# One hybrid encoder layer on one Trainium2 core: orders in the VectorE and ScalarE queues of the gated-attention stage and of the merge

## The chip, the cores and the metric

One core of a Trainium2 chip. The metric is the device time of one execution in microseconds (us), lower is better. TensorE is called PE in the profile, its weight loads PEld; VectorE is DVE, ScalarE is ACT, GpSimd is POOL; SyncE (SP) issues most of the transfers.

## The reference

One layer over 1088 tokens (1024 of a prompt, 64 of a running stream) of width 1024. The three branches share one projection of the normalised input; only branches B and C and the merge are touched here.

```python
u = rmsnorm(x, g) @ w_in            # q, k, v, low-rank gate, output gate r, memory q, merge gates
# B: gated linear attention, 4 heads, dk=64, dv=128, blocks of 64 tokens
b = cumsum(log_a); q_d = q*exp(b); k_d = k*exp(-b); k_e = k*exp(b_last - b)
o = tril(q_d @ k_d.T) @ v + q_d @ S
S = exp(b_last) * S + k_e.T @ v     # from block to block
o_gla = rmsnorm_per_head(o) * g * silu(r)
# C: softmax attention of 4 heads x 128 into 256 memory tokens; K, V = rmsnorm(mem) @ w
h = x + w_out( sum over 3 branches of sigmoid(gate_n) * (o_n @ w_branch[n]) )
# then a router, two experts of 32 for each token (top 2 of 8 in the best of 4 groups), final rmsnorm
```

All products run in fp32 accuracy. A large product takes three passes: each operand is split into a high part (a copy on ACT, `w_high`, `x_high`) and a low part (a subtraction on DVE, `w_low`), and PE adds low x high, high x low and high x high (`three_pass`, L68).

## The kernel before

The kernel is a chain of stages, each with five instruction queues written out by hand and tied by counting semaphores (`wait_ge`, `then_inc`); a queue runs strictly in the order in which it is written. This case touches the joint stage of branches B and C (from 358 to 733 us of the profiled execution) and the start of the merge stage (from 733 us).

**Joint stage.** The four heads of branch B are done as two pairs p = 0 and 1. Columns of the projection come in blocks of 128 (`BLOCKS`: q, k, v, v for each pair, then r0 to r3, then mq, mk, mv for each memory head), and each block b is split into units of 384, 384 and 320 tokens (`units`, 0 to 40 and more). A unit is 24 matmuls of PE into one half of `gproj`; it waits until DVE has the low half of its weights (`g_low`, by `w_low(b)`) and until ACT has emptied the unit two before it (`drained`). ACT's `take` drains units, and after the last unit of block b it splits the high half of block b + 2 (`w_high`, L1140); after the last unit of an r block it also runs `sigmoid`, three activations over 1088 columns (L1218 to L1222). DVE's `w_low` is L1314.

For each pair ACT's `grow(p)` (L1187 to L1193) turns the scanned log-decay into three tiles `tt`, `la`, `bs` and the block factors `dec`; DVE's `gate_q` (L1338) and `gate_k` (L1344, L1346) multiply them into q and k, giving `qd`, `kd` and `ke`. PE transposes `ke` and v (`turn`, L949), DVE copies the results out (L1356). Then `stream(p)` runs t = 0 to 8 over tiles of 128 tokens: `pair` (L962) and `update` (L973) on PE for t + 1, DVE's `mask` (L1367) and `advance` (L1380), and `attend` (L987, L993). Units of later blocks are threaded between them by `PRE`, `MID` and `POST`; for pair 1: unit 30, the column sums `squares` (L1001) and unit 31 at t = 4, unit 32 after it; unit 33 at t = 6; unit 34, squares, unit 35 at t = 8. Before each `squares` ACT must `evacuate` the outputs (L1199) and square them (L1205); after it `root` (L1210, L1213) and DVE's `norm` (L1388) finish the head norm. `silu(h)` on DVE (L1394, L1397) uses the sigmoid of r; drains of r2 and r3 wait for the `silu` of r0 and r1, whose tiles they overwrite. The memory rows are normalised by `memory_norm` on ACT and DVE (L1431), transposed on PE by `memory_rows` (L1027) behind stream(1), split by `memory_high` (L1247) and `memory_low` (L1437); behind `memory_rows` PE goes on with unit 36 (block 12, the first memory query).

Queue order before, as far as it is touched:

- ACT: stream(0), grow(1), unit 18's drain, ...; in stream(1) each sigmoid directly after the last drain of its r block, so sigmoid(0) at t = 1, sigmoid(1) at t = 3, sigmoid(2) at t = 4, sigmoid(3) at t = 8 in front of `w_high(13)`; memory_norm at t = 2 and 3; then evacuate(1, 2) and memory_high.
- DVE: stream(0) ending in norm(0, 1), then w_low(7), gate_q(1), gate_k(1); in stream(1) silu(0), silu(1), silu(2) at t = 3, 4, 6, memory_norm at t = 6, 7, norm(1, 1) at its end; then memory_low, w_low(12), w_low(13).
- grow(1) also waits until all state updates of pair 0 are done, since both pairs use one tile `dec`.

**Merge stage.** Step i = 0 to 23 covers branch n = i // 8 and 128 output columns: PE's `gate(i)` (three groups of 24 matmuls, `bank<-xhi,...`) and `part(i)` (three groups of 12), DVE's `weigh(i, g)` (L2230), ACT's `sigmoid(i)` (L2045, one activation for each group). The gate of step 0 was computed in the joint stage. PE runs gate(1), part(0), part(1), gate(2), part(2), ...; gate(2) waits for DVE's w_low(2) and for sigmoid(1), which empties its banks. In ACT's queue sigmoid(1) stands behind `w_high(2)` (L2025) and `wb_high(2)` (L2030), and wb_high(2) waits for a transfer that SP issues only when part(0) is done (L1722). At the same time POOL writes 8 MB of zeros to `expert_rows` (16 transfers of 512 KB, L1767).

Of the kernel before, what the change touches and what calls it, by code (L numbers as in the profile page):

```python
# [13 lines left out]
F32 = mybir.dt.float32  # L14
# [4 lines left out]
ACT = mybir.ActivationFunctionType  # L19
# [57 lines left out]
def build(nc, io, stop_after=99):  # L77
# [709 lines left out]
    G, E = [la, bs], [tt, qr]  # L787
    SM = CON + 2560
    NCH = T // CH
    dec = at("dec", [P, NCH], F32, SM)  # L790
    gnt = at("gnt", [P, 4], F32, SM + 96)
    bat = at("bat", [P, 2], F32, SM + 128)
    cmask = at("cmask", [P, P], I32, SM + 192)
    w2c = [at("w2c", [RANK, P], F32, off) for off in (SM + 704, CON + 512)]
    PRE = [{4: [14], 8: [16]}, {4: [30], 8: [34]}]
# [3 lines left out]
    with ExitStack() as own, Stage(nc) as ctx:  # L799
# [335 lines left out]
        def _(act):  # L1135
# [49 lines left out]
            def grow(p):  # L1185
                act.wait_ge(scanned, p + 1)
                nc.scalar.activation(tt[:, :], bs[:, :], ACT.Exp, scale=1.0 / TAU)  # L1187
                if p:
                    act.wait_ge(advanced, NCH)
                nc.scalar.activation(dec[:, :], blk(bs[:, :])[:, :, CH - 1], ACT.Exp, scale=1.0 / TAU)  # L1190
                nc.scalar.activation(la[:, :], la[:, :], ACT.Exp, scale=1.0 / TAU)
                act.drain()
                nc.scalar.activation(bs[:, :], bs[:, :], ACT.Exp, scale=-1.0 / TAU).then_inc(grown, 1)  # L1193
# [30 lines left out]
            def take(js):  # L1224
                for j in js:
                    drain(j)
                    b = units[j][0]
                    if j + 1 == done[b]:
                        if BLOCKS[b][0] == "r":
                            sigmoid(BLOCKS[b][1])  # L1230
                        if b + 2 < len(BLOCKS):
                            w_high(b + 2)

            def memory_norm(t):
                act.wait_ge([row0, row1][t], 16)
# [33 lines left out]
            def stream(p):  # L1269
                for t in range(NT):  # L1270
                    if t in (4, 8):
                        evacuate(p, t // 4 - 1)
                    take(PRE[p].get(t, []))
                    if t in (4, 8):
                        root(p, t // 4 - 1)
                    take(MID[p].get(t, []))
                    take(POST[p].get(t, []))
                    if p and t in (2, 3):
                        memory_norm(t - 2)
                if p == 0:  # L1280
                    evacuate(p, 2)

            w_high(0)
            w_high(1)
# [5 lines left out]
            softplus(1)  # L1290
            take(range(9, 13))
            stream(0)
            grow(1)
            take([18])
            root(0, 2)
            take(range(19, 24))
            stream(1)
            evacuate(1, 2)
            for t in range(2):
                memory_high(t)  # L1300
            take([36])
            root(1, 2)
            take(range(37, 41))
# [4 lines left out]
        def _(ve):  # L1308
# [29 lines left out]
                nc.vector.tensor_tensor(qd[:, :], qr[:, :], tt[:, :], ALU.mult).then_inc(qd_ready, 1)  # L1338

            def gate_k(p):  # L1340
                ve.wait_ge(drained, first["k", p] + 3)
                if p:
                    ve.wait_ge(paired, NT)
                nc.vector.tensor_tensor(kd[:, :], ke[:, :], bs[:, :], ALU.mult).then_inc(kd_ready, 1)  # L1344
                ve.drain()
                nc.vector.tensor_tensor(ke[:, :], ke[:, :], la[:, :], ALU.mult).then_inc(ke_ready, 1)  # L1346
# [23 lines left out]
            def advance(p, t):  # L1370
                ve.wait_ge(updated, 9 * p + t + 1)
                if t == FULL:
                    ve.wait_ge(st_in, 16 * p + 16)
                if p and t == 0:
                    ve.wait_ge(stored, 32)
                for u in range(rows_of(t) // CH):
                    c = 2 * t + u
                    src, dst = (c, c + 1) if c < 16 else (17, 18)
                    ve.drain()
                    nc.vector.scalar_tensor_tensor(out=S[:, dst, :], in0=S[:, src, :], scalar=dec[:, c:c + 1],  # L1380
                                                   in1=half(ub, u)[:, 0:P], op0=ALU.mult, op1=ALU.add).then_inc(advanced, 1)

            def norm(p, g):
# [23 lines left out]
            def stream(p):  # L1407
                mask(p, 0)
                advance(p, 0)
                for t in range(NT):  # L1410
                    if t + 1 < NT:
                        mask(p, t + 1)
                        advance(p, t + 1)
                    if t == 4 and p == 0:
                        w_low(6)
                    if p:
                        if t in (2, 4):
                            w_low(9 + t // 2)
                        if t in (3, 4, 6):
                            silu({3: 0, 4: 1, 6: 2}[t])  # L1420
                    if t == 5:
                        norm(p, 0)
                    if p and t in (6, 7):
                        memory_norm(t - 6)
                norm(p, 1)

            def memory_norm(t):
                ve.wait_ge(mrooted, t + 1)
# [74 lines left out]
                copy(0, kind, g)  # L1503
            w_low(5)
            stream(0)
            w_low(7)
            gate_q(1)
            gate_k(1)
            for kind, g in (("k", 0), ("k", 1), ("k", 2)):
                copy(1, kind, g)  # L1510
            w_low(8)
# [4 lines left out]
            stream(1)  # L1516
            for t in range(2):
                memory_low(t)
            w_low(12)
            w_low(13)  # L1520
            silu(3)
            norm(1, 2)
            w_low(14)
# [138 lines left out]
    with Stage(nc) as ctx:  # L1662
# [358 lines left out]
        def _(act):  # L2021
# [74 lines left out]
            for i in range(LEAD):  # L2096
                if i % KC == 0:
                    o_split(i // KC)
                if i:
                    w_high(i + 1)  # L2100
                wb_high(i + 1)
                if LEAD - 2 <= i:
                    wo_split(2 * (i - LEAD + 2))
                    wo_split(2 * (i - LEAD + 2) + 1)
                if i:
                    sigmoid(i)
            w_high(LEAD + 1)
            wb_high(LEAD + 1)
# [477 lines left out]
```

## Time and profile before

| | |
|---|---|
| median of 3 runs | 1951.29 us (1948.56 to 1953.52) |
| the profiled execution | 1949.11 us, its span 1947.5 us |
| PE busy | 1784.2 us (92% of the span), 10344 matmuls |
| DVE, ACT, POOL busy | 1105.5 us (57%), 874.9 us (45%), 193.4 us (10%) |
| mean granted PE clock | 0.961 of full speed |
| transfers | 326.57 MB, mean 168 GB/s |

The span in 40 slices of 48.7 us, busy share in tenths; the joint stage lies in slices 8 to 15, the merge begins at slice 16:

```profile
PE   7998898899998998999999999969999999999960
...
DVE  4328777443234542223233335557888988898857
ACT  4215545323243432112121223236887788778832
...
PEclk9999999899999998999999999979999999999985
```

Timeline rows read: start in us, duration (of a merged run of xN instructions, first start to last end), engine, line, operation, output <- inputs, shapes; in brackets the idle time in front of it and what ended it.

### The profile page before, as it was taken

What the parts mean: (1) busy time and instruction counts of PE and PEld (TensorE: products, weight loads), DVE (VectorE), ACT (ScalarE), POOL (GpSimd) and SP (SyncE); (2) the same over time, 40 slices, a digit from 0 to 9 for tenths busy, and PEclk for the clock granted to TensorE, in tenths of its full rate; (3) what the DMA queues carried; (4) which work ended last, traced back from release to release, by engine and by line L of the source; (5) the groups of instructions that cost most, each with busy time, mean ns of one, the idle gap of its engine ahead of it and who ended that gap; (6) DMA issues with size and microseconds to landing.
All of it is one profiled execution on the core that took longest, in us unless ns stands there. A gap on an engine that the chain in (4) does not pass through costs nothing. (4 is left out here: it accounts for less than half of the span.)

```text
span 1947.5 us, 25714 instructions
## 1 busy us (share of the span) xinstructions
PE 1784.2 (92%) x10344; PEld 1570.7 (81%) x10344; DVE 1105.5 (57%) x1343; ACT 874.9 (45%) x1128; POOL 193.4 (10%) x189
## 2 busy tenths in 40 slices
PE   7998898899998998999999999969999999999960
PEld 5877777687977877999999998857888888888850
DVE  4328777443234542223233335557888988898857
ACT  4215545323243432112121223236887788778832
POOL 0004445100000003000000000000000000000003
PEclk9999999899999998999999999979999999999985
DMA  4210000111101217111112142149999999999947
GB/s 173 81 58 24 23 23 1 46 33 48 44 25 55 82 39 220 49 49 44 39 49 88 47 148 76 71 160 349 417 410 415 415 417 408 417 415 411 403 159 273
DMA packets 131719, 326.57 MB, mean 168 GB/s; under 512 B 8576, under 2 KB 84176, under 8 KB 107024
## 3 DMA queue, kind: packets, MB, share of 16 engines
q1 hardware_dynamic: 116096, 269.40, 37.0%
q0 software_dynamic: 10896, 38.74, 5.5%
q10 hardware_dynamic: 4608, 16.78, 2.1%
q8 instruction: 84, 1.38, 0.3%
q14 instruction: 35, 0.29, 0.0%
HBM read 285.01 MB, written 39.87 MB: 167 GB/s over the span
## 5 line engine op out<-in xcount | busy, mean ns | idle before, releaser
L2320 DVE TENSOR_TENSOR low<-raw,hig 128x2048 fp32r<-128x2048 f32 x192 | 431.5, 2286 | 68.1 <-ACT hig L2092 67.7
L2092 ACT ACTIVATE hig<-raw 128x2048 fp32r<-128x2048 f32 x192 | 359.5, 1915 | 21.9 <-ACT ye L2160 14.2
L1945 PE MATMUL bank<-hig,xel 128*128 128x512 f32 x512 | 204.4, 399 | 3.9 <-DVE xel L2387 3.9
L1947 PE MATMUL bank<-hig,xeh 128*128 128x512 f32 x512 | 201.6, 394 | 0.0
L1946 PE MATMUL bank<-low,xeh 128*128 128x512 f32 x512 | 200.9, 392 | 0.0
L71 PE MATMUL bank<-xhi,glo 128*128 128x384 f32 (+1 forms) x552 | 181.3, 329 | 9.5 <-ACT sg L2045 7.8
L72 PE MATMUL bank<-xlo,ghi 128*128 128x384 f32 (+1 forms) x552 | 181.2, 328 | 0.0
L73 PE MATMUL bank<-xhi,ghi 128*128 128x384 f32 (+1 forms) x552 | 181.1, 328 | 0.0
L71 PE MATMUL gproj<-xhi,glo 128*128 128x384 f32 (+1 forms) x408 | 142.4, 349 | 10.1 <-DVE glo L1314 10.1
L73 PE MATMUL gproj<-xhi,ghi 128*128 128x384 f32 (+1 forms) x408 | 136.9, 335 | 0.0
L72 PE MATMUL gproj<-xlo,ghi 128*128 128x384 f32 (+1 forms) x408 | 136.8, 335 | 0.0
L672 DVE TENSOR_TENSOR_SCAN sfx<-sfx 128x1024 f32<-128x1024 f32 (+8 forms) x68 | 116.7, 1739 | 4.3 <-ACT sfx L547 4.1
L1945 PEld LDWEIGHTS bank<-hig,xel 128*128 128x128 f32 x512 | 97.6, 191 | 23.6 <-DVE xel L2387 4.5
L1947 PEld LDWEIGHTS bank<-hig,xeh 128*128 128x128 f32 x512 | 96.9, 189 | 20.7
L1946 PEld LDWEIGHTS bank<-low,xeh 128*128 128x128 f32 x512 | 97.3, 190 | 19.2
L71 PEld LDWEIGHTS bank<-xhi,glo 128*128 128x128 f32 x552 | 104.4, 189 | 9.9 <-issue 9.9
L284 POOL TENSOR_TENSOR att<-att,sfx 128x1023 f32<-128x1023 f32 (+8 forms) x68 | 98.6, 1461 | 117.3 <-DVE sfx L672 87.7
L2234 DVE TENSOR_TENSOR tm<-sg,bank 128x384 f32<-128x384 f32 (+1 forms) x42 | 22.3, 532 | 153.9 <-PE bank L73 153.9
L1971 PE MATMUL bank<-hig,htl 128*128 128x512 f32 x256 | 103.3, 403 | 1.4 <-DVE htl L2393 1.4
L73 PEld LDWEIGHTS bank<-xhi,ghi 128*128 128x128 f32 x552 | 104.5, 189 | 0.0
L72 PEld LDWEIGHTS bank<-xlo,ghi 128*128 128x128 f32 x552 | 104.4, 189 | 0.0
L1973 PE MATMUL bank<-hig,hth 128*128 128x512 f32 x256 | 100.6, 393 | 0.0
(403 smaller groups left out, 3630.5 us busy)
## 6 DMA issues: line engine op xcount, KB each, us to landing
raw<-in_w_e_gate_dram SPq DMA_DIRECT2D x64, 1024.0 KB, 8.0
raw<-in_w_e_up_dram SPq DMA_DIRECT2D x64, 1024.0 KB, 8.3
raw<-in_w_e_down_dram SPq DMA_DIRECT2D x64, 1024.0 KB, 7.5
graw<-in_w_in_dram SPq DMA_DIRECT2D x40, 512.0 KB, 3.6
expert_rows<-ye ACTq DMA_DIRECT2D x32, 512.0 KB, 8.2
xt<-in_x_prompt_dram SPq DMA_DIRECT2D x16, 512.0 KB, 3.6
expert_rows<-nil POOLq DMA_DIRECT2D x16, 512.0 KB, 10.3
braw<-in_w_branch_dram SPq DMA_DIRECT2D x24, 256.0 KB, 2.7
```

Source lines behind the costliest of these rows:

```text
L71: nc.tensor.matmul(out, wl, xh, start=(i == 0), stop=False)
L72: nc.tensor.matmul(out, wh, xl, start=False, stop=False)
L73: last = nc.tensor.matmul(out, wh, xh, start=False, stop=(i == len(parts) - 1))
L284: nc.gpsimd.tensor_tensor(att[n][:, 0:k - 1], att[n][:, 0:k - 1], sfx[n][:, 1:k], ALU.mult).then_inc(weighed, 1)
L672: nc.vector.tensor_tensor_scan(v, v, v, 1.0, ALU.mult, ALU.bypass).then_inc(scanned, 1)
L1945: nc.tensor.matmul(bank[:, :], xel[n % 2][:, kk, :], wh[:, k, :], start=(kk == 0), stop=False)
L1946: nc.tensor.matmul(bank[:, :], xeh[n % 2][:, kk, :], wl[:, k, :], start=False, stop=False)
L1947: last = nc.tensor.matmul(bank[:, :], xeh[n % 2][:, kk, :], wh[:, k, :], start=False, stop=(kk == KC - 1))
L1971: nc.tensor.matmul(bank[:, :], htl[n % 2][:, kk, :], wh[:, k, cols], start=(kk == 0), stop=False)
L1973: last = nc.tensor.matmul(bank[:, :], hth[n % 2][:, kk, :], wh[:, k, cols], start=False, stop=(kk == 3))
L2092: nc.scalar.activation(hig[q % HI][:, :], raw[q % RAW][:, :], ACT.Copy).then_inc(high, 1)
L2320: nc.vector.tensor_tensor(low[q % RAW][:, :], raw[q % RAW][:, :], hig[q % HI][:, :].bitcast(F32), ALU.subtract).then_inc(lowed, 1)
```

## The change

`dec` gets a slot for each pair and grow(1) loses its wait; grow(1) moves from behind stream(0) into it, at t = 4. On DVE gate_k(1) comes first behind stream(0), then norm(0, 1), gate_q(1), w_low(7). In stream(1) the sigmoids come at t = 1, 4 (between unit 31's and unit 32's drains) and 5, the fourth behind memory_high; ACT's memory_norm at t = 5 and 6; DVE's silu at t = 3, 6, 7, w_low(12) at t = 7, memory_norm at t = 7, 8, and norm(1, 1) behind w_low(13). In the merge w_high(2) and sigmoid(1) are issued in step 0, in front of wb_high(2).

```diff
-    dec = at("dec", [P, NCH], F32, SM)
-    gnt = at("gnt", [P, 4], F32, SM + 96)
-    bat = at("bat", [P, 2], F32, SM + 128)
+    dec = at("dec", [P, 2, NCH], F32, SM)
+    gnt = at("gnt", [P, 4], F32, SM + 160)
+    bat = at("bat", [P, 2], F32, SM + 1216)
...
-                if p:
-                    act.wait_ge(advanced, NCH)
-                nc.scalar.activation(dec[:, :], blk(bs[:, :])[:, :, CH - 1], ACT.Exp, scale=1.0 / TAU)
+                nc.scalar.activation(dec[:, p, :], blk(bs[:, :])[:, :, CH - 1], ACT.Exp, scale=1.0 / TAU)
...
-                    if j + 1 == done[b]:
-                        if BLOCKS[b][0] == "r":
-                            sigmoid(BLOCKS[b][1])
-                        if b + 2 < len(BLOCKS):
-                            w_high(b + 2)
+                    if j + 1 == done[b] and b + 2 < len(BLOCKS):
+                        w_high(b + 2)
...
+                    if p and t == 4:
+                        sigmoid(1)
                     take(POST[p].get(t, []))
-                    if p and t in (2, 3):
-                        memory_norm(t - 2)
-                if p == 0:
-                    evacuate(p, 2)
+                    if p == 0 and t == 4:
+                        grow(1)
+                    if p and t in (1, 5):
+                        sigmoid(t // 2)
+                    if p and t in (5, 6):
+                        memory_norm(t - 5)
+                evacuate(p, 2)
...
             stream(0)
-            grow(1)
...
             stream(1)
-            evacuate(1, 2)
             for t in range(2):
                 memory_high(t)
+            sigmoid(3)
             take([36])
...
             def gate_k(p):
+                ve.wait_ge(grown, p + 1)
...
+                        if t == 7:
+                            w_low(12)
-                        if t in (3, 4, 6):
-                            silu({3: 0, 4: 1, 6: 2}[t])
+                        if t in (3, 6, 7):
+                            silu({3: 0, 6: 1, 7: 2}[t])
                     if t == 5:
                         norm(p, 0)
-                    if p and t in (6, 7):
-                        memory_norm(t - 6)
-                norm(p, 1)
+                    if p and t in (7, 8):
+                        memory_norm(t - 7)
...
             stream(0)
+            gate_k(1)
+            norm(0, 1)
+            gate_q(1)
             w_low(7)
-            gate_q(1)
-            gate_k(1)
...
             for t in range(2):
                 memory_low(t)
-            w_low(12)
             w_low(13)
+            norm(1, 1)
             silu(3)
...
-                if i:
+                if i >= 2:
                     w_high(i + 1)
                 wb_high(i + 1)
...
-                if i:
+                if i == 0:
+                    w_high(2)
+                    sigmoid(1)
+                elif i >= 2:
                     sigmoid(i)
```

## Rows read from the trace of the kernel before

**Rows 1.** Waits of TensorE (PE), 355 to 860 us: reader <- writer: total, times, longest us.

```profile
PE gproj L71 <- DVE glo L1314: 12.0, 5, 7.2
PE bank L71 <- ACT sg L2045: 7.8, 1, 7.8
PE gupd L949 <- DVE ke L1346: 4.1, 1, 4.1
PE gout L1001 <- ACT osq L1205: 3.6, 1, 3.6
...
PE gout L1046 <- DVE pT L1462: 2.8, 2, 2.0
```

**Rows 2.** Windows, TensorE alone: us, busy (instructions), granted clock, DMA share, GB/s.

```profile
486.00:549.00 63.00, 60.59 (x426) 1.00 0.15 43
...
766.00:768.00 2.00, 2.00 (x8) 0.50 1.05 384
...
726.00:727.00 1.00, 0.68 (x5) 1.00 0.00 0
```

**Rows 3.** Timeline of ScalarE (ACT), 463 to 479 us: start, us, instruction [idle before <-releaser].

```profile
463.73 1.03 ACT L1199 ACTIVATE o_gla<-gout 128x1024 f32<-128x1024 f32 x1 [6.57 <-PE gout L993]
...
473.34 0.44 ACT L1175 ACTIVATE ke<-gproj 128x320 f32<-128x320 f32 x1 [1.27 <-PE gproj L73]
...
475.18 1.10 ACT L1187 ACTIVATE tt<-bs 128x1088 f32<-128x1088 f32 x1
...
477.47 1.11 ACT L1193 ACTIVATE bs<-bs 128x1088 f32<-128x1088 f32 x1
```

**Rows 4.** Timeline of VectorE (DVE), 472 to 485 us.

```profile
472.11 1.42 DVE L1388 SCALAR_TENSOR_TENSOR o_gla<-o_gla,gnt,osq 128x512 f32<-128x512 f32 x2 [9.21 <-ACT osq L1213]
...
481.21 1.29 DVE L1346 TENSOR_TENSOR ke<-ke,la 128x1088 f32<-128x1088 f32 x1
...
483.48 1.20 DVE L1356 COPY ken<-gupd 128x384 f32<-128x384 f32 x2 [0.98 <-PE gupd L949]
```

**Rows 5.** Timeline of PE, 485 us: column sums of pair 0, last group.

```profile
484.85 0.95 PE L1001 MATMUL gout<-osq,ones 128*128 128x64 f32 x4
```

**Rows 6.** Timeline of ACT, 543 to 553 us.

```profile
543.46 0.44 ACT L1175 ACTIVATE bs<-gproj 128x320 f32<-128x320 f32 x1 [3.59 <-PE gproj L73]
...
551.05 1.06 ACT L1205 ACTIVATE osq<-o_gla 128x1024 f32<-128x1024 f32 x1
```

**Rows 7.** Timeline of PE, 560 to 582 us.

```profile
560.83 0.61 PE L987 MATMUL gout<-atm,gvn 128*128 128x128 f32 x4
...
579.96 1.88 PE L1001 MATMUL gout<-osq,ones 128*128 128x512 f32 x4
```

**Rows 8.** Timeline of PE, 595 to 602 us.

```profile
595.17 0.69 PE L71 MATMUL gproj<-xhi,glo 128*128 128x384 f32 x1 [7.15 <-DVE glo L1314]
...
601.03 0.55 PE L1001 MATMUL gout<-osq,ones 128*128 128x64 f32 x4
```

**Rows 9.** Timeline of PE, 764 to 785 us, merge stage.

```profile
764.72 0.66 PE L71 MATMUL bank<-xhi,glo 128*128 128x384 f32 x1 [7.81 <-ACT sg L2045]
...
784.69 0.34 PE L71 MATMUL bank<-xhi,glo 128*128 128x384 f32 x1
```

**Rows 10.** Timeline of ACT, 763 to 777 us, merge stage.

```profile
763.57 0.63 ACT L2030 ACTIVATE bhi<-braw 128x512 fp32r<-128x512 f32 x1 [21.78 <-DMA braw<-in_w_branch_dram]
...
775.50 1.06 ACT L2025 ACTIVATE ghi<-graw 128x1024 fp32r<-128x1024 f32 x1 [10.22 <-DMA graw<-in_w_in_dram]
```

**Rows 11.** Timeline of DVE, 776 us, merge stage.

```profile
776.59 1.22 DVE L2208 TENSOR_TENSOR glo<-graw,ghi 128x1024 fp32r<-128x1024 f32 x1 [9.97 <-ACT ghi L2025]
```

**Rows 12.** Timeline of SyncE's DMA issues (SPq), 784 to 803 us, merge stage.

```profile
784.89 0.37 SPq L1722 DMA_DIRECT2D braw<-in_w_branch_dram  x1
...
796.75 0.37 SPq L1713 DMA_DIRECT2D graw<-in_w_in_dram  x1
...
802.69 0.37 SPq L1722 DMA_DIRECT2D braw<-in_w_branch_dram  x1
```

More of the change, by code:

```diff
@@ L1379, in advance @@
                     ve.drain()
-                    nc.vector.scalar_tensor_tensor(out=S[:, dst, :], in0=S[:, src, :], scalar=dec[:, c:c + 1],
+                    nc.vector.scalar_tensor_tensor(out=S[:, dst, :], in0=S[:, src, :], scalar=dec[:, p, c:c + 1],
                                                    in1=half(ub, u)[:, 0:P], op0=ALU.mult, op1=ALU.add).then_inc(advanced, 1)
```

## Prediction

> **What bounds the kernel now.** I read the page first: PE is busy 92% of the span, so time can be won only where PE stands still or runs at the lower clock. The waits of PE from the joint stage into the merge come next [rows 1]: four of them are single holes of 3.6 to 7.8 us, released by DVE's `ke`, ACT's `osq`, DVE's `glo` and ACT's `sg`; the other waits there are 2 us or less. The windows say what a hole costs beside itself [rows 2]: after the one of 7.8 us the granted clock is 0.50 (1.2 GHz), while behind an idle time of 2.0 us in the last memory head, and through 63 us with only small waits, it stayed at 1.00 (2.4 GHz). Last I read the timelines of ACT and DVE around each hole, to see what stood in the queue in front of the releasing instruction. In each sum, x is the moment that PE would reach with the change, on the clock of the old trace.
>
> The prices that recur: an activation over 1088 columns 1.1 us, so a sigmoid of three with its drains or `grow` some 3.4 us (475.18 to 478.58 [rows 3]); a DVE multiply over 1088 columns 1.29 us and two norms 1.42 us [rows 4]; `w_low` 1.22 us [rows 11]; `w_high` 1.06 us [rows 10]; a gate of 1088 columns 11.86 us and a part 5.94 us [rows 12], so a unit of 384 columns 11.86 x 384 / 1088 = 4.19 us.
>
> **Term a, the gates of pair 1.** PE has finished unit 18 at 478.4 (`ke` ready at 481.21 + 1.29 = 482.5, less the hole of 4.1 [rows 1, 4]). In front of `ke` stand grow(1) on ACT and norm, w_low(7), gate_q and kd on DVE. grow(1) moves into ACT's idle 6.57 us before evacuate(0, 1), which begins at 463.73 [rows 3]: it fits with 3.1 us to spare, and its scan lies in front of pair 0's whole stream in DVE's queue. Giving `dec` a second slot costs nothing; it only removes the wait. gate_k(1) then waits for the last k drain alone, 473.34 + 0.44 = 473.8 [rows 3], and `ke` is ready at 473.8 + 2 x 1.29 + 0.1 = 476.5, 1.9 us before PE wants it. What is late next: the third transpose group needs DVE's first copy, which now stands behind norm, gate_q and w_low(7), 1.42 + 1.29 + 1.22 less small overlaps: the copy starts at 480.3 where it started at 483.48 [rows 4]. That leaves a hole of some 1.5 us at 479.2, of the size that did not cost the clock. The gain is 3.2 us, plus 0.4 us for the column sums (0.95 us [rows 5] where the same form took 0.55 us [rows 8]), plus my estimate of 0.5 us for the transposes and first matmuls, which ran at the lower clock too. **4.1 us**; bounds 2.5 (the clock falls all the same) and 4.6.
>
> **Term b, the first column sums of pair 1.** PE went on at 551.05 + 1.06 = 552.1 after a hole of 3.6 us, so unit 30 ended at 548.5 [rows 1, 6]. In front of that square ACT had sigmoid(1), w_high(11), memory_norm(1) and the evacuation copy. With the sigmoid gone to after unit 31's drain, and the memory norm to t = 6, ACT drains unit 29 by 543.9 [rows 6], splits until 544.9, copies and squares until 547.1: 1.4 us before PE wants it. Then x = 548.5 + 1.88 (sums at full clock [rows 7]) + 4.19 (unit 31) = 554.6, where attend(4) began at 560.83 [rows 7]. **6.3 us**; bounds 0, if the 1.4 us are not there, and 6.5.
>
> What moves behind it must stay covered. By the same durations laid behind one another, sigmoid(0) ends near 532 and its silu near 542, before unit 30's drain needs it at 548.5. sigmoid(1) ends 3.4 us after unit 31's drain, near 558.5 on PE's new time; silu(1) stands behind mask(7) and advance(7), and ends near 566.4, while unit 33, whose drain needs it, ends near 567.3. sigmoid(2), memory_norm on both engines and w_low(12) follow in the holes; the mrow transposes are reached near 579.4 and their norms end near 573.6. No SP issue moves except by PE's own progress, and POOL's queue is untouched.
>
> **Term c, unit 36.** PE stopped at 595.17 - 7.15 = 588.0 and reached the next column sums at 601.03 [rows 8]; the unit alone takes 4.19 us, so 1.7 us of the 13.0 were the lower clock. The hole is a chain behind unit 35's drain: sigmoid(3) 3.4 us, w_high(13) 1.06, evacuation, four memory_high, four memory_low, w_low(12). w_low(12) now runs at t = 7 on DVE, more than 10 us before unit 36, and unit 36 needs nothing else of the chain. The three units of block 12 (11.9 us) then cover memory_high and memory_low (about 5 us), w_low(13) 1.2, norm(1, 1) 1.4 and silu(3). x = 588.0 + 4.2 = 592.2. **8.8 us**; bounds 5 and 9.
>
> **Term d, the merge.** PE stopped at 764.72 - 7.81 = 756.9 [rows 9]. sigmoid(1) stood behind wb_high(2), whose weights landed at 763.57 [rows 10]. Issued before it, sigmoid(1) waits only for weigh(0, g) and ends near 752; wb_high(2), now behind it, waits for the same transfer as before. gate(2) and part(2) then run from 756.9 to 756.9 + 11.86 + 5.94 = 774.7. What is late next is gate(3)'s weight block: landed at 775.50 [rows 10], low half ready at 776.59 + 1.22 = 777.8 [rows 11]. Its transfer is issued when part(0) is done, before anything changes, so it does not come earlier. gate(3) begins at 777.8 instead of 784.69 [rows 9]: 6.9 us. The new hole of 3.1 us lies between 2.0 (clock kept) and 3.6 us (sums of 3.78 us for 1.88, clock lost); nearest the latter, so I charge it what the old hole cost: 784.69 - 764.72 - 17.80 = 2.2 us. **4.7 us**; bounds 0 and 6.9.
>
> A rule of the Trainium skill would give another result here. The row shows that behind wb_high(2)'s block (763.57) the 512 KB of gate(3) took 12 us more, some 44 GB/s, while all queues together moved 384 [rows 2, 10]. DMA: Bandwidth & Descriptors, Queues, rings and completion order, says that each DMA engine takes the queue rows with work in turn, packet by packet. With an even share, 192 GB/s, the block would land 2.7 us after 763.57, gate(3) would not wait, and term d would be 7.8 + 2.2 = 10.0 us. The trace speaks against the even share, and I keep 4.7.
>
> **The sum.** 4.1 + 6.3 + 8.8 + 4.7 = 23.9 us. The profiled execution took 1949.11 us, so 1925.2; it lies 2.2 us under the median 1951.29, and against the median I get 1927.4 us. What follows (rest of the merge, router, experts) is released by PE's progress and moves forward whole; its first weights are ordered by PE's counts, not by a clock. A measurement of this kernel tells 0.3%, 5.9 us, from no change.
>
> **Rivals.**
> 1. One covered step is not covered. Term b has 1.4 us to spare, silu(1) has 0.9 us before unit 33's drain (and 1.5 us more before squares(1, 1) would feel it). If one fails by enough to take a hole of over 3 us, about 6 us are lost: 1933.5. For: the slacks are thin. Against: they are sums of steady durations. 0.15.
> 2. The merge gives nothing back: gate(3)'s transfer lands later, or the hole moves whole to gate(3): 1951.3 - 19.2 = 1932.1. 0.06.
> 3. The even share of the rule above: 1927.4 - 5.3 = 1922.1. For: only the rule. Against: rows 10. 0.04.
> 4. The saved time is not on the path: what bounds the later stages is their weight stream, and the stage's end only waits there. 1951. Against: those loads begin only when PE's projections of the merge are done. 0.05.
> 5. Slower: without its rests PE runs densely through the stage and is granted 1.2 GHz for longer. The first matmul of a gate took 0.66 us at 0.50 and 0.34 us at 1.00 [rows 2, 9]; at half the clock a stretch of dense work takes up to twice its time. It decides from some 30 us of work at that level, which cost the 24 gained and the 5.9 that a measurement tells; over the 55 us of PE work between the holes of terms b and c and the first memory head it would be 55 us: 1982. Against: the 63 us before the hole of term b ran at 1.00 with PE busy for 60.6 of them [rows 2]. 0.03.
>
> The forecast itself has 0.67. The range 1921 to 1935 takes in rivals 1 to 3 and the bounds of terms a and d; it leaves out 4, 5 and a failure of two terms. Faster by over 0.3%: 0.92; within: 0.05; slower: 0.03.
>
> **What would show it.** In the changed kernel's waits of PE: `ke` gone or under 0.5 us, `ken` at about 1.5 us, `osq` gone, the 7.15 us of `glo` gone, `sg` gone, and a new `glo` L2208 hole of about 3 us at gate(3) with the clock at 0.50 behind it. The joint stage should be 19 us shorter (358 to 733 before), gate(4) should begin 4.7 us earlier in the merge, and everything after should keep its length. Wrong if an `osq` or `bs` drain wait of over 3 us appears near 545 to 575, or if gate(3)'s wait is near 8 us or missing.

## The result and the profile after

The changed kernel takes 1925.3 us (median of 4 runs, 1921.16 to 1928.22) against 1951.2 us: ratio 0.9864, interval 0.9846 to 0.9883, so 26.5 us faster (22.8 to 30.0). The profiled execution took 1926.25 us, its span 1924.8 us, the mean granted clock is 0.967 (0.961 before).

The waits of PE from 355 to 860 us, to be read against [rows 1] (reader <- writer: total, times, longest in us):

```profile
PE gproj L71 <- DVE glo L1313: 4.9, 4, 2.9
...
PE bank L71 <- ACT sg L2047: 3.4, 1, 3.4
PE gout L1046 <- DVE pT L1463: 2.9, 2, 2.0
...
PE gupd L949 <- DVE ken L1356: 2.1, 2, 1.7
```

`ke` and `osq` are gone. What is left of `glo` (L1313 is the old L1314) is 2.9 us at the stage's start, before anything that the change touches, and three small ones. New are 1.7 us at `ken`, inside the 2.1, and 3.4 us at `sg` where 7.8 stood. That label does not say that sigmoid(2) is the cause: it stands in ACT's queue behind the splits of gate(3)'s and part(3)'s weights, and the timelines below show that ACT itself had waited for a transfer.

Pair 1's gates on DVE, the queue of [rows 4] in its new order:

```profile
473.02 1.29 DVE L1344 TENSOR_TENSOR kd<-ke,bs 128x1088 f32<-128x1088 f32 x1 [10.94 <-ACT ke L1175]
...
478.14 1.22 DVE L1313 TENSOR_TENSOR glo<-graw,ghi 128x1024 fp32r<-128x1024 f32 x1
...
479.28 1.01 DVE L1356 COPY ken<-gupd 128x384 f32<-128x384 f32 x2
```

`kd` starts when k has been drained, and `ke` (behind it, at 474.41) is ready at 475.7, before PE goes over from unit 18 to the transposes at 477.45. The copies of the transposed `ke` begin at 479.28, behind w_low(7); that is the new hole. On PE (the rows of the third transpose group, the column sums of pair 0 and 1, attend(4), and the sums behind unit 36):

```profile
479.98 0.52 PE L949 MATMUL gupd<-ident,ke 128*128 128x128 f32 x3 [1.71 <-DVE ken L1356]
...
480.33 0.56 PE L1001 MATMUL gout<-osq,ones 128*128 128x64 f32 x4
...
546.41 1.88 PE L1001 MATMUL gout<-osq,ones 128*128 128x512 f32 x4
...
552.29 0.61 PE L987 MATMUL gout<-atm,gvn 128*128 128x128 f32 x4
...
583.51 0.55 PE L1001 MATMUL gout<-osq,ones 128*128 128x64 f32 x4
```

To be compared with [rows 5, 7, 8]: the sums at 480.33 take 0.56 us for 0.95; the sums of pair 1 run at 546.41 without a wait, in 1.88 us; from there to attend(4) it is 5.9 us, before it was 12.2 from the end of unit 30; and the sums behind unit 36 come 4.2 us after the last memory transposes, before 13.0.

The merge, against [rows 9 to 12], in four timelines: ACT's weight splits for part(2) and gate(3); DVE's low half for gate(3); PE's start of gate(3); and SP's issues when part(1), part(2) and gate(3) are done.

```profile
745.93 0.63 ACT L2032 ACTIVATE bhi<-braw 128x512 fp32r<-128x512 f32 x1 [11.48 <-DMA braw<-in_w_branch_dram]
...
758.07 1.06 ACT L2027 ACTIVATE ghi<-graw 128x1024 fp32r<-128x1024 f32 x1 [11.51 <-DMA graw<-in_w_in_dram]
```

```profile
759.16 1.23 DVE L2213 TENSOR_TENSOR glo<-graw,ghi 128x1024 fp32r<-128x1024 f32 x1 [10.19 <-ACT ghi L2027]
```

```profile
760.44 0.44 PE L71 MATMUL bank<-xhi,glo 128*128 128x384 f32 x1 [3.39 <-ACT sg L2047]
```

```profile
739.28 4.22 SPq L1724 DMA_DIRECT2D braw<-in_w_branch_dram  x1
...
757.08 0.37 SPq L1724 DMA_DIRECT2D braw<-in_w_branch_dram  x1
...
774.14 0.37 SPq L1715 DMA_DIRECT2D graw<-in_w_in_dram  x1
```

The issues at 739.28 and 757.08 mark the ends of part(1) and part(2): gate(2) and part(2) now take 17.80 us, as two steps of that kind without a hole did before. gate(3) waits for weights that land at 758.07, 24.3 us after their issue at 733.75; their low half is ready at 759.16 + 1.23 = 760.39, and gate(3) starts at 760.44.

The granted clock shows what the prediction had not counted. Windows of the changed kernel, then two of the kernel before, at and behind the head of stream(1), which begins at 504.4 us in the one and at 507.9 in the other (us, PE's busy time, granted clock, DMA share, GB/s):

```profile
482.00:484.00 2.00, 2.00 (x8) 0.50 0.00 0
484.00:486.00 2.00, 2.00 (x10) 0.74 0.00 0
508.00:510.00 2.00, 2.00 (x18) 0.73 0.04 8
510.00:512.00 2.00, 2.00 (x8) 0.50 0.00 0
```

```profile
508.00:512.00 4.00, 2.21 (x28) 1.00 0.47 131
512.00:516.00 4.00, 4.00 (x29) 1.00 0.02 4
```

Behind the 1.7 us hole the clock is 1.2 GHz again near 482 to 485 us, and once more near 509 to 512 us, behind the small holes at the head of stream(1), where it had held in the profile before.

### The profile page after: what moved, and what is told of

Its sections match the earlier page's. It is cut to its first block and busy times, and to the rows that moved or that the text cites. A ratio compares the mean times of both kernels' runs of the same rounds, so it can differ in the third digit from the quotient of the medians.

```text
span 1924.8 us, 25715 instructions
## 1 busy us (share of the span) xinstructions
PE 1778.6 (92%) x10344; PEld 1566.6 (81%) x10344; DVE 1107.9 (58%) x1343; ACT 878.2 (46%) x1128; POOL 211.2 (11%) x189
## 5 line engine op out<-in xcount | busy, mean ns | idle before, releaser
L1800 POOL DMA_INDIRECT xe<-ffn_rows,toks x32 | 62.0, 1937 | 463.0 <-PE bank L1933 455.6
```

Source lines behind the costliest of these rows:

```text
L1800: pool.indirect_dma_start(xe[n % 2][:, :], None, htd, bass.IndirectOffsetOnAxis(ap=toks[:, n:n + 1], axis=0)).then_inc(fetched[n % 2], 16)
```

## The experiments

Eleven kernels, each with one profile. For all of them the table gives what PE did in the joint stage (from the first projection matmul to the merge's first) and in the first 100 us of the merge. Idle is the stretch less PE's busy time; "clock" is the busy time times (1 - granted clock), added up over windows of 1 us, so the time that the lower clock cost. Length less idle less clock is 325 to 326 us in the joint stage of every kernel.

| kernel | median us (runs) | ratio to before, interval | joint stage us: length, idle, clock | merge us: idle, clock |
|---|---|---|---|---|
| before | 1951.2 (4) | 1 | 365.6, 27.1, 12.5 | 7.8, 2.3 |
| changed | 1925.3 (4) | 0.9864, 0.9846 to 0.9883 | 348.1, 13.8, 9.3 | 3.4, 1.7 |
| gates only | 1949.9 (10) | 0.9993, 0.9981 to 1.0006 | 365.9, 24.6, 15.8 | 7.7, 2.2 |
| stream only | 1939.0 (4) | 0.9938, 0.9921 to 0.9954 | 356.5, 16.4, 15.1 | 7.3, 3.1 |
| merge only | 1946.9 (8) | 0.9983, 0.9969 to 0.9998 | 368.1, 27.0, 15.7 | 3.0, 0.0 |
| w_low(12) late | 1931.9 (4) | 0.9912, 0.9890 to 0.9934 | 352.7, 17.4, 9.7 | 3.7, 1.7 |
| copies first | 1927.6 (4) | 0.9884, 0.9865 to 0.9904 | 349.9, 12.9, 12.1 | 3.1, 1.4 |
| zeros late | 1922.4 (4) | 0.9845, 0.9827 to 0.9864 | 349.0, 14.3, 9.6 | 0.0, 0.0 |
| w_low behind masks | 1921.6 (4) | 0.9851, 0.9829 to 0.9873 | 341.1, 12.1, 3.2 | 3.2, 3.0 |
| all three | 1914.7 (5) | 0.9816, 0.9801 to 0.9831 | 341.2, 11.1, 4.4 | 0.0, 0.0 |
| before, w_low behind masks | 1946.1 (12) | 0.9966, 0.9952 to 0.9981 | 362.6, 25.5, 11.2 | 7.3, 2.4 |
| the same with gates | 1943.8 (6) | 0.9947, 0.9926 to 0.9968 | 357.6, 22.8, 9.1 | 7.8, 2.3 |
| changed, without gates | 1933.0 (6) | 0.9902, 0.9882 to 0.9922 | 356.5, 16.4, 15.1 | 3.3, 3.0 |

The three groups of experiments (the first four, the next four, the last three) ran on three different chips; the kernel before measured 1949.7, 1951.4 and 1952.3 us beside them. The ratios take that out, and where kernels of different groups are compared below, the ratios decide. The clock columns come from one execution each, so a difference of 3 us in them is within what two executions of one code showed (see the merge alone).

### The parts alone

**The gates** (kernel before plus this):

```diff
-                if p:
-                    act.wait_ge(advanced, NCH)
-                nc.scalar.activation(dec[:, :], ...
+                nc.scalar.activation(dec[:, p, :], ...
...
+                    if p == 0 and t == 4:
+                        grow(1)
...
             stream(0)
+            gate_k(1)
+            norm(0, 1)
+            gate_q(1)
             w_low(7)
-            gate_q(1)
-            gate_k(1)
```

> The kernel before with the gate part alone: two slots of dec, grow(1) inside stream(0), gate_k(1) first on VectorE, norm(0, 1) and gate_q(1) and w_low(7) behind it. Theory (the four holes are independent and each part removes its own): the 4.1 us hole at ke goes, a hole of 1.7 us at ken comes, joint stage 4.1 us shorter (bounds 2.5 and 4.6), time about 1947. Rival (the saved time is given back at the next hole, since the squares of pair 1 wait for ScalarE work that is not earlier): the osq hole grows from 3.6 to over 6 us and the time stays at 1951.

Measured: 1.4 us less by the ratio (from 3.7 less to 1.2 more), so the 4.1 us are not there. The theory's holes are: its waits of PE

```profile
PE gout L1001 <- ACT osq L1203: 3.6, 1, 3.6
...
PE gupd L949 <- DVE ken L1356: 2.1, 2, 1.7
```

show no `ke`, 1.7 us of `ken`, and `osq` at 3.6 us as before, so the rival, which had the time return as a longer `osq` hole, fails. Idle falls by 2.5 us. In this profile the clock column takes it back: 15.8 for 12.5 us, with a stretch at the lower level from 508 to 515 us that the profile before did not have (windows, columns as above). Behind the hole at `ken` itself, the same 1.7 us as in the changed kernel, the clock did not fall here.

```profile
510.00:514.00 4.00, 4.00 (x19) 0.50 0.00 0
```

**The order of stream(1) and what follows** (kernel before plus the edits of `take`, `stream(1)`, `silu`, `w_low(12)`, `norm(1, 1)` and `sigmoid(3)`):

```diff
+                    if p and t == 4:
+                        sigmoid(1)
...
+                    if p and t in (1, 5):
+                        sigmoid(t // 2)
+                    if p and t in (5, 6):
+                        memory_norm(t - 5)
...
+                        if t == 7:
+                            w_low(12)
+                        if t in (3, 6, 7):
+                            silu({3: 0, 6: 1, 7: 2}[t])
```

> The kernel before with the order of stream(1) and what follows it alone: sigmoids, silus, memory norms, w_low(12), norm(1, 1), and neither the gate part nor the merge part. Theory: the holes at osq (3.6 us) and in front of unit 36 (7.15 us) go, the one at ke (4.1 us) and the one in the merge (7.8 us) stay as they are; joint stage 15.1 us shorter, time about 1936. Rival (one of the two needs the earlier gates as well): only one of them goes, 1942 to 1945.

Measured: 0.9938, 12.1 us less (9.0 to 15.4), at the upper end of which lies the forecast of 15.1. Both holes go, and idle falls by 10.7 us, which is 3.57 + 7.15. The rival that one of them needs the earlier gates fails: waits of PE,

```profile
PE bank L71 <- ACT sg L2047: 7.3, 1, 7.3
PE gproj L71 <- DVE glo L1314: 4.9, 4, 2.9
PE gupd L949 <- DVE ke L1346: 4.1, 1, 4.1
```

with `glo` at 4.9 and 2.9 us as in the changed kernel. Here too the clock gives 2.6 us back (15.1 for 12.5).

**The merge** (kernel before plus the merge's lines):

```diff
-                if i:
+                if i >= 2:
                     w_high(i + 1)
...
+                if i == 0:
+                    w_high(2)
+                    sigmoid(1)
+                elif i >= 2:
                     sigmoid(i)
```

> The kernel before with the second gate's sigmoid in front of wb_high(2) alone. Theory: the 7.8 us hole at sg goes, one of 3.1 to 3.4 us at gate(3) comes, which is the transfer of gate(3)'s weights behind the zeros; merge 4.7 to 4.9 us shorter, joint stage as before, time about 1946.5. Rival (even share of the transfers): no hole at gate(3), 10 us gained, 1941.

Measured: 0.9983, 3.3 us less (0.4 to 6.0), within it the 4.7 forecast. The hole at gate(3) is there and the rival of the even share fails. In this profile, unlike the changed kernel's, the hole did not bring the lower clock (ACT's split for gate(3), PE's wait, and a window of PE behind it):

```profile
777.56 1.06 ACT L2025 ACTIVATE ghi<-graw 128x1024 fp32r<-128x1024 f32 x1 [11.51 <-DMA graw<-in_w_in_dram]
```

```profile
PE bank L71 <- ACT sg L2045: 3.0, 1, 3.0
```

```profile
780.00:784.00 4.00, 3.92 (x23) 1.00 0.08 23
```

So a hole of 3.0 us cost its own length here and one of 3.4 us cost 1.7 us more there. The joint stage, whose code is the old one, was 2.5 us longer in this profile than in the one before, all of it in the clock column.

The idle times are additive: 2.5 + 10.7 + 4.8 = 18.0 us for the parts, 13.3 + 4.4 = 17.7 us for the whole. The measured times are not: the parts add up to 0.86%, 16.8 us (uncertain by some 0.25%, the root of the squared half intervals), the whole gives 1.36%, 26.5 us. In the profiles it is the clock that does not add up: over both stretches of the table its column rises by 3.2, 3.4 and 0.9 us in the three parts and falls by 3.8 us in the whole. Why the lower clock returned in the parts is open.

**w_low(12) put back** behind the four `memory_low`, all else as changed:

```diff
-                        if t == 7:
-                            w_low(12)
...
                 memory_low(t)
+            w_low(12)
             w_low(13)
```

> The changed kernel with w_low(12) alone put back behind the four memory_low. Theory (term c is one chain, and both the sigmoid and the place of w_low(12) are in it): sigmoid(3) no longer holds the chain, but unit 36 waits until 582.9 where TensorE is ready at 579.3, a hole of 3.6 us and some 2 us of lower clock, 5.5 us slower than the changed kernel, about 1931. Rival (the sigmoid in front of w_high(13) was the whole cause): no hole, the time of the changed kernel, 1925.

Measured: 1931.9 us, ratio 0.9912, so 6.6 us over the changed kernel by the medians and 9.4 by the ratios (intervals apart). The profile has the very hole: `glo` has one more wait, of 3.5 us, idle is 3.6 us higher, and the clock is low behind it at 581 to 585 us.

```profile
PE gproj L71 <- DVE glo L1313: 8.4, 5, 3.5
```

The rival fails. Of term c's hole of 7.15 us, 3.5 return with w_low(12)'s old place alone. The other 3.65 us belong to the other moves; a sigmoid takes 3.4 us, so that sigmoid(3)'s place holds them is likely, but it was not put back alone.

### What is left in the changed kernel

**Copies first**:

```diff
             gate_k(1)
             norm(0, 1)
-            gate_q(1)
-            w_low(7)
             for kind, g in (("k", 0), ("k", 1), ("k", 2)):
                 copy(1, kind, g)
+            gate_q(1)
+            w_low(7)
```

> The changed kernel with VectorE's three copies of the transposed ke put in front of gate_q(1) and w_low(7), behind norm(0, 1). Theory (the 1.7 us hole at ken is what the two steps cost, and a hole of that size already brings the lower clock near 482 us): the hole falls to 0.1 us, the low stretch at 481 to 485 us goes, 1.7 us of idle and 1.7 us of clock gained, about 1922. Rival (the low stretches come at any place whatever the holes): 1.7 us gained and the low stretch is there again, near 1923.5.

Measured: 1927.6 us, no gain (0.9884 against 0.9864, the intervals overlap). The hole is gone (`ken` 0.8 us in two waits, 0.4 the longest) and so is the low clock at 481 to 485 us (PE's wait, then windows):

```profile
PE gupd L949 <- DVE ken L1356: 0.8, 2, 0.4
```

```profile
482.00:484.00 2.00, 2.00 (x15) 1.00 0.00 0
506.00:508.00 2.00, 2.00 (x8) 0.50 0.00 0
708.00:710.00 2.00, 2.00 (x3) 0.50 0.03 8
```

but the stretch at the head of stream(1), 504 to 511 us, is twice as long as in the changed kernel, and behind the 2.0 us hole of the last memory head stands a stretch at 705 to 712 us that the changed kernel's profile did not have. Idle fell by 0.9 us and the clock column, 12.1 for 9.3, took it back. Neither theory nor rival as written: the hole went, the time did not follow. Nor does the missing low stretch at 482 us show that the hole had caused it: of the six profiles that have the 1.7 us hole at `ken`, only two have the lower clock behind it (changed, w_low(12) late), and four do not (gates only, zeros late, w_low behind masks, and gates with w_low behind masks).

**Zeros late**:

```diff
             nc.gpsimd.memset(nil[:, :], 0.0)
             pool.drain()
+            pool.wait_ge(b_in[1], 32)
             with pool.Fori(0, OVER) as b:
```

> The changed kernel with GpSimd's 16 transfers of zeros issued only once the weights of part(3), and so those of gate(3), have landed. Theory (the 3.4 us hole at gate(3) is the transfer of its weights queued with the zeros): gate(3)'s weights land within 5 us of their issue instead of 24, the hole goes with the low clock behind it, 3.4 to 5.1 us gained, about 1920.5. Rival 1 (the hole moves on: the weights of gate(4) are issued among the zeros and now come late): a hole of 3 us or more at gate(4), 1925. Rival 2 (the transfer is slow for another reason): it still takes over 15 us, 1925.

Measured: 1922.4 us (0.9845; 3.7 us of ratio under the changed kernel's, intervals overlapping). The merge has no idle time and no low clock in its first 100 us. ACT's splits of the weights of gate(3) and gate(4):

```profile
741.03 1.06 ACT L2028 ACTIVATE ghi<-graw 128x1024 fp32r<-128x1024 f32 x1 [1.06 <-DMA graw<-in_w_in_dram]
...
772.00 1.06 ACT L2028 ACTIVATE ghi<-graw 128x1024 fp32r<-128x1024 f32 x1 [17.24 <-DMA graw<-in_w_in_dram]
```

gate(3)'s weights are split at 741.03, 4.1 us after their issue at 736.93 where it was 24.3 us, and 22.6 us after the merge's first matmul at 718.48; in the changed kernel it was 42.8 us after it (758.07 and 715.27). Rival 1 is right in its first half: gate(4)'s weights now come late, at 772.00 behind 17.2 us of waiting on ACT, but PE needs them only after part(3), and the only wait at `bank` that is left is the 1.7 us in front of the merge's first matmul, which the kernel before has too. Rival 2 fails: it was the zeros.

**w_low behind the masks**:

```diff
-            w_low(5)
             stream(0)
...
-            w_low(9)
             stream(1)
...
                 for t in range(NT):
                     if t + 1 < NT:
                         mask(p, t + 1)
                         advance(p, t + 1)
+                    if t == 0:
+                        w_low(5 + 4 * p)
```

> The changed kernel with w_low(5) and w_low(9) moved from in front of stream(0) and stream(1) to behind VectorE's second advance in them. Theory (the small holes of 1.1 us at atm in both pairs are the mask queued behind w_low, and such a cluster of small holes brings the lower clock near 431 and 508 us): both atm holes fall to some 0.3 us, 1.6 us of idle gained and up to 3.4 to 5 us of clock, 1919 to 1923.5. Rival (low stretches are tied to nothing on the engine): 1.6 us gained, and low stretches stand at both places, 1923.5.

Measured: 1921.6 us (0.9851), the profiled execution 1919.3. Idle falls by 1.7 us and the clock column from 9.3 to 3.2 us: the joint stage is 7.0 us shorter. Windows of PE over the places of the two old stretches, which began near 430 and 509 us:

```profile
424.00:440.00 16.00, 15.11 (x154) 1.00 0.01 2
500.00:516.00 16.00, 16.00 (x120) 1.00 0.00 1
```

In the profile the rival fails: there is no low stretch at either place. The time does not decide: against the changed kernel it is 3.7 us by the medians and 2.5 us by the ratios, inside the noise, and both the theory's range and the rival's 1923.5 lie in the spread of the four runs (1917.6 to 1925.3).

**All three together.**

> The changed kernel with all three: copies first, zeros late, w_low behind the masks. Theory: idle time of TensorE from 355 to 860 us falls by 1.7 + 3.4 + 1.6 = 6.7 us and the low clock with it, 8 to 12 us faster than the changed kernel, 1913 to 1917. Rival (holes closed are replaced by low clock elsewhere, or the waits move on): not more than 4 us faster, 1921 or more.

Measured: 1914.7 us (5 runs, 1914.44 to 1917.99), ratio 0.9816, interval 0.9801 to 0.9831: 35.9 us under the kernel before and 9.4 us of ratio under the changed one. It beats both, and its interval lies outside the changed kernel's. PE's waits from 355 to 860 us, the longest three:

```profile
PE gproj L71 <- DVE glo L1313: 4.9, 4, 2.9
PE gpair L915 <- DMA w2c<-in_w_gla_a_dram: 3.6, 1, 3.6
PE gout L1046 <- DVE pT L1465: 2.9, 2, 2.0
```

and no hole over 2.0 us is left behind the stage's start. By the ratios the three alone add up to 2.3 us, less than the whole's 9.4 but with an uncertainty as large as the difference, so how the 9.4 us divide among them is open. The two first waits are the largest that remain: 3.6 and 2.9 us at the stage's start, 3.4 and 2.9 in the kernel before (`PE gpair L915 <- DMA w2c` and `glo`), with the clock at 1.2 GHz from about 361 to 374 us around them. No run here touches them.

### The gate part again

Since the gates alone had given next to nothing, they were added to, and taken from, kernels with other holes. First the kernel before with only the diff of "w_low behind the masks":

> The kernel before with w_low(5) and w_low(9) alone moved behind VectorE's second advance in stream(0) and stream(1). Theory (the cluster of small holes at the head of each stream brings a stretch of lower clock behind it): no low clock near 434 and 510 us, 1.7 us of idle and 1.7 to 5 us of clock gained against the kernel before, ratio 0.9965 to 0.998. Rival (what the same move gained in the changed kernel needed its other holes closed): ratio 0.999 or more.

Measured: 0.9966 (0.9952 to 0.9981), 6.6 us (3.7 to 9.4) for 1.6 us of idle. No low clock near 434 and 510 us in its profile. The rival fails. The two profiles show less of it, a joint stage 3.0 us shorter and a clock column 1.3 us lower; the profile of the kernel before had only the first of the two low stretches.

Then that with the gates' diff as well:

> The same with the gate part added (two slots of dec, grow(1) in stream(0), gate_k(1) first). Theory (the gate part takes 2.4 us of idle for good, and alone it gained nothing because the lower clock near 508 us gave the rest back): ratio 0.002 below that of the kernel with w_low alone, and no low clock near 508 us. Rival (the gate part is worth nothing, its hole only moves to ken and to the small holes of stream(1)): the same ratio as with w_low alone, within 0.0007.

Measured: 0.9947 against 0.9966, the 0.002 of the theory, though the two intervals overlap. Its second half fails: the clock was low from 507 to 515 us in this profile:

```profile
508.00:512.00 4.00, 4.00 (x18) 0.50 0.02 4
```

And the changed kernel with the gates' diff taken back:

> The changed kernel without the gate part, so the order of stream(1) and the merge part alone. Theory (the gate part is worth its idle time, 2.4 us, and some clock): 2.4 to 4.1 us slower than the changed kernel, 1928 to 1929.5, ratio 0.9876 to 0.9884. Rival (worth nothing here either): ratio 0.9864 as with the whole change.

Measured: 0.9902 (0.9882 to 0.9922) against 0.9864, so 7.4 us slower without the gates, more than forecast, and the intervals just overlap. The rival that they are worth nothing here fails by its own number.

The idle time that the gate part takes is the same in all three pairs: 27.1 to 24.6, 25.5 to 22.8, 16.4 to 13.8 us, so 2.5 to 2.7. The times that go with them are 1.4, 3.7 and 7.4 us of ratio (0.0007, 0.0019, 0.0038), each uncertain by about 2.5 to 5 us. So the idle part is shown to be the same in each. That the whole price differs is not shown: anything from 2.1 to 3.7 us lies in all three intervals, and the forecast 4.1 just above the first of them. The clock column moves by +3.3, -2.1 and -5.8 us in the three pairs, and with one profile for each kernel it is open whether that is the kernel or the execution.

## Why the prediction was right

It said 1927.4 us, and 1925.2 for the profiled execution by its own sum; the runs gave 1925.3 and the profiled execution 1926.25. The mechanism was right: the four named holes went, each released by what had been moved, and the two new ones came where they were said to come. One price was wrong, and two differences that no term contains nearly cancelled. By its steps:

**Term a, 4.1 us.** From the end of unit 18 to the end of the column sums it was 7.4 us and is 3.4: 4.0 us, with `ke` at 475.7 (forecast 476.5) and the copy at 479.28 (480.3, on a trace that runs 0.9 us earlier there). But these 4.0 us end before the clock falls at 482 us. Counted from the end of unit 18 to the next transposes, of v (PE; before, then after), it was 497.75 - 478.45 = 19.3 us and is 494.23 - 477.45 = 16.8:

```profile
497.75 0.82 PE L949 MATMUL gupd<-ident,vT 128*128 128x128 f32 x6
```

```profile
494.23 0.82 PE L949 MATMUL gupd<-ident,vT 128*128 128x128 f32 x6
```

So in this profile term a gave 2.5 us, its lower bound ("the clock falls all the same"), and the step "a hole of some 1.5 us, of the size that did not cost the clock" failed: the hole measured 1.7 us, and the lower clock behind it cost 1.7 us. That a hole of 2.0 us in the last memory head had kept the clock [rows 2] was one case, taken for a rule: behind the same hole the clock fell in seven of the eleven experiments' profiles (the window at 708 us above is one). Behind the 1.7 us hole it fell in two of six.

**Term b, 6.3 us.** Measured 12.2 - 5.9 = 6.3 us. The square ended at 543.81 + 1.06 = 544.9, 1.5 us before PE wanted it (forecast 1.4):

```profile
541.45 0.44 ACT L1175 ACTIVATE bs<-gproj 128x320 f32<-128x320 f32 x1 [5.26 <-PE gproj L73]
...
543.81 1.06 ACT L1203 ACTIVATE osq<-o_gla 128x1024 f32<-128x1024 f32 x1
```

Of the covered steps, silu(1) ended at 564.1 and unit 33's drain, which needs it, began at 565.53: 1.4 us of slack for the 0.9 forecast. Rival 1 did not come.

**Term c, 8.8 us.** Measured 13.0 - 4.2 = 8.8 us. w_low(12) ran at 566.45, 12.8 us before unit 36. The run with w_low(12) put back shows that it was a member of the chain, and that the other moves had taken the rest.

**Term d, 4.7 us.** From part(1)'s end to gate(3)'s end it was 796.75 - 756.94 = 39.8 us and is 774.14 - 739.28 = 34.9: 4.9 us. The hole at gate(3) was 3.4 us for 3.1, and it brought the lower clock, as the sum charged. Rival 3, the even share of the transfers, did not come: 24.3 us for 512 KB beside the zeros, and without the zeros beside them the same weights came in time. The block's 512 KB took 12.1 us, from 745.93 to 758.07, some 43 GB/s, if they moved behind the block before them.

The prediction took that even share for what a rule of the Trainium skill gives. The page (DMA: Bandwidth & Descriptors, Queues, rings and completion order) says that an engine takes the queues' packets in turn; that each queue then gets as many bytes is not in it. This trace shows no such thing either: the zeros' packets, as the profile counts them, are 3.6 KB and those of the loads 0.5 KB, so that from 746 to 758 us (packets, MB, share of the 16 engines; q0 has the zeros, q1 the loads)

```profile
q0 software_dynamic: 904, 3.27, 73.9%
q1 hardware_dynamic: 1784, 0.90, 26.3%
```

the loads had the larger part of the packets and a fifth of the bytes. The turns themselves no run here tests.

**The sum.** With term a at 4.0 us the four terms measure 24.0 us, forecast 23.9; with term a at 2.5 they measure 22.5, and the two spans differ by 22.7. That this is so close is in part luck. The joint stage is 17.6 us shorter, which is 2.5 + 6.3 + 8.8, but two more differences lie in it. At the head of stream(1), from its first `pair` to the end of unit 30, the changed kernel takes 1.4 us more, with the new low stretch at 509 us; and up to the end of unit 18 it takes 0.8 us less, with the same code: the profile before has a low stretch at 401 us that the changed kernel's does not have (PE alone, a window of before), and a shorter one near 430 us.

```profile
400.00:402.00 2.00, 2.00 (x9) 0.67 0.00 0
```

By the table, idle fell by 13.3 us, of which the holes of a, b and c are 2.4 + 3.6 + 7.15, but the clock only by 3.2 us, where the terms had counted on some 6 beside their holes. That the medians then differ by 26 us, more than the profiled pair, is within the intervals.

One reading of the rows was wrong, without effect on the sum: besides the four holes there were two more of over 2 us in the stretch, at the stage's start and left alone by the change, the 2.9 us inside `glo`'s 12.0 and

```profile
PE gpair L915 <- DMA w2c<-in_w_gla_a_dram: 3.4, 1, 3.4
```

Rivals 2, 4 and 5 did not come either: the merge kept its gain, the later stages only moved forward (from 100 us into the merge to the end, 1114.5 and 1109.5 us, the difference being term d), and the joint stage's clock did not stay at 1.2 GHz.

The forecast rested on the holes being independent. For the idle time that is shown by the parts run alone. For the time it is not: the gates alone gave 1.4 us (at most 3.7) where the sum had 4.1, and the three parts alone 16.8 us where the whole gave 26.5. The sum of independent terms met the whole and not the parts; that it met the whole is to that extent luck.

## What to carry to other kernels

In a kernel of handwritten queues, list the holes of the engine that bounds, and for each ask what stands in front of the releasing instruction in its queue and what in there is needed that early: here four such reorderings without one instruction less gave 1.4%, and three more moves found in the changed kernel's own profile another 0.5%. Work out the slack of each thing moved on the new timetable; slacks forecast at 1.4 and 0.9 us came out at 1.5 and 1.4. Price a hole at its length, and expect the clock to add to it, but do not read what it adds from one profile: behind one and the same hole it fell in some executions and not in others. A cluster of small holes may deserve the first attention.

## What the runs showed of the hardware

The lower clock does not need a hole of 3 us, and what it does behind a short one varies. In the thirteen profiles, from 355 to 830 us:

- Behind every hole of 3.1 us or more it was low; behind the one of 3.0 us (merge alone) it was not.
- Behind the 2.0 us hole of the last memory head it was low in seven of thirteen, behind the 1.7 us hole at `ken` in two of six.
- Behind the cluster of holes of 0.3 to 1.1 us at the head of stream(0) it was low in all nine profiles in which w_low(5) stands in front of the first masks, and in none of the four in which it stands behind them. At the head of stream(1) it was low in eight of the nine (the profile before is the exception) and in one of the four (507 to 514 us).
- Near 401 to 406 us it was low in four of thirteen (before, gates only, zeros late, before with w_low behind masks) though PE had no idle time in the 25 us in front.

Such a stretch cost 1.7 or 3.4 us in most cases, so that two executions of one joint stage can differ by 3 us, as the merge-only run's did.

Moving two VectorE instructions of 1.2 us out from in front of the first masks, worth 1.6 to 1.7 us of idle, made the kernel before 6.6 us (3.7 to 9.4) faster, and the changed kernel's profiled joint stage 7.0 us shorter (2.5 us by the ratio of the times, not clear of noise). That the cluster at a stream's head brings the low clock is well supported by nine of nine against none of four, and for stream(1) less so. Which part of the cluster it is, and what exactly the chip reacts to, was not tried.

A transfer of 512 KB that took 24.3 us from issue to landing beside POOL's zeros took 4.1 us when the zeros were held back, and the next block, now issued among them, was split 17.7 us after its issue at 754.32.
